# A sixth slot in the ring of split weights, and splitting five units ahead, in a two-layer hybrid decoder on one core

## The reference, cut to what matters

```python
for layer in range(2):
    h = rms_norm(x, attn_norm)
    proj = h @ w_in          # 1024 x 7428: pool, diff q k v, stick q k v, forgetting q k v, forget, gates
    o_pool, o_diff, o_sb, o_fox = mixers(proj)        # o_sb: stick-breaking attention
    merged = sum(sigmoid(gate_n + b_gate_n) * (o_n @ w_branch[rows_n]) for n in range(4))
    x = x + merged @ w_out
    h = rms_norm(x, ffn_norm)
    gate, up = split(h @ w_up)                         # 2 * 2816 columns
    x = x + (silu(gate) * up) @ w_down
```

## Time and profile before

| | |
|---|---|
| median of 3 runs | 895.01 us (894.31 to 897.45) |
| the profiled execution, whole | 895.68 us |
| its span, first to last instruction | 892.8 us |
| TensorE busy | 875.3 us, 98% |
| VectorE, ScalarE, GpSimd busy | 611.1, 443.0, 114.4 us |
| mean granted TensorE clock | 0.994 |
| DMA | 160.10 MB, mean 179 GB/s |

### The profile page before, as it was taken

How to read it: one execution, slowest core, us unless ns; L and a number is a source line. 1 busy time by engine, 2 the same in 40 slices (tenths; PEclk the granted TensorE clock), 3 DMA queues, 4 the chain that set the end, 5 groups by cost and what they waited for, 6 DMA issues and landing times.

```text
span 892.8 us, 11371 instructions
## 1 busy us (share of the span) xinstructions
PE 875.3 (98%) x4308; PEld 722.3 (81%) x4308; DVE 611.1 (68%) x902; ACT 443.0 (50%) x635; POOL 114.4 (13%) x89
## 2 busy tenths in 40 slices
PE   7998999999999999999999989999999999999998
PEld 6876888788788888888888878887887888888886
DVE  5799677777967666654478977758687676666542
ACT  5464654654445444443274645546444554444431
POOL 0553000001800010000005510000045000000000
PEclk9999999999999999999999989999999999999999
DMA  8843755475566766555555346454656466666551
GB/s 272 268 124 97 225 165 167 130 236 188 187 194 195 213 186 184 183 183 193 183 165 170 115 124 209 137 181 145 235 180 201 146 213 189 189 188 189 181 196 47
DMA packets 91014, 160.10 MB, mean 179 GB/s; under 512 B 11472, under 2 KB 17744, under 8 KB 90960
## 3 DMA queue, kind: packets, MB, share of 16 engines
q1 hardware_dynamic: 90960, 159.38, 57.3%
HBM read 158.31 MB, written 1.05 MB: 179 GB/s over the span
## 4 chain that ended last, share of the span: by engine, by line
PE 81%; DVE 13%; issue 2%; DMA 1%; ACT 1%; POOL 1%; SPq 0%; POOLq 0%; DVEq 0%; ACTq 0%
PE bulk L1591 24%; PE bulk L1595 24%; PE bulk L1592 24%; DVE w_lo L941 6%; DMA raw<-in_w_in_dram 1%; PE bankAB L1346 1%; POOL wide L667 1%; PE bankT L1486 1%; ACT w_hi L695 1%; DVE wide L1240 1%; DVE stat L1027 1%; DVE wide L1039 1%; PE bankAB L1532 1%; PE bankO L1505 1%; DVE softplus_lo L1110 0%
## 5 line engine op out<-in xcount | busy, mean ns | idle before, releaser
L941 DVE TENSOR_TENSOR w_lo<-raw,w_hi 128x1024 fp32r<-128x1024 f32 (+1 forms) x288 | 368.4, 1289 | 165.9 <-ACT w_hi L695 163.4
L695 ACT ACTIVATE w_hi<-raw 128x1024 fp32r<-128x1024 f32 (+1 forms) x288 | 299.7, 1049 | 259.7 <-PE bulk L1595 232.5
L1591 PE MATMUL bulk<-w_hi,hT_hi 128*128 128x512 f32 (+1 forms) x896 | 354.0, 395 | 3.7 <-DVE w_lo L941 3.6
L1592 PE MATMUL bulk<-w_lo,hT_hi 128*128 128x512 f32 (+1 forms) x896 | 346.8, 387 | 0.0
L1595 PE MATMUL bulk<-w_hi,hT_lo 128*128 128x512 f32 (+1 forms) x896 | 343.7, 388 | 0.0
L1591 PEld LDWEIGHTS bulk<-w_hi,hT_hi 128*128 128x128 f32 x896 | 169.3, 189 | 38.7 <-DVE w_lo L941 5.1
L1595 PEld LDWEIGHTS bulk<-w_hi,hT_lo 128*128 128x128 f32 x896 | 168.7, 189 | 34.6
L1592 PEld LDWEIGHTS bulk<-w_lo,hT_hi 128*128 128x128 f32 x896 | 169.5, 189 | 32.1
L1591 PE MATMUL bulk<-w_hi,aT_hi 128*128 128x512 f32 x176 | 68.8, 391 | 0.0
L1595 PE MATMUL bulk<-w_hi,aT_lo 128*128 128x512 f32 x176 | 68.5, 389 | 0.0
L1592 PE MATMUL bulk<-w_lo,aT_hi 128*128 128x512 f32 x176 | 68.5, 389 | 0.0
(11 more groups left out here) (240 smaller groups left out, 737.1 us busy)
## 6 DMA issues: line engine op xcount, KB each, us to landing
raw<-in_w_in_dram SPq DMA_DIRECT2D x112, 512.0 KB, 4.0
raw<-in_w_ffn_up_dram SPq DMA_DIRECT2D x80, 512.0 KB, 4.4
raw<-in_w_ffn_down_dram SPq DMA_DIRECT2D x44, 512.0 KB, 3.3
raw<-in_w_branch_dram SPq DMA_DIRECT2D x20, 512.0 KB, 3.3
raw<-in_w_out_dram SPq DMA_DIRECT2D x16, 512.0 KB, 3.2
bias<-in_b_gate_dram SPq DMA_DIRECT2D x16, 256.0 KB, 4.0
raw<-in_w_ffn_up_dram SPq DMA_DIRECT2D x16, 256.0 KB, 3.1
raw<-in_w_in_dram SPq DMA_DIRECT2D x8, 256.0 KB, 2.6
```

The lines of the kernel that those rows point to most:

```text
L695: act.activation(w_hi[:, g % RING, :, 0:width], raw[:, g % RAW, :, 0:width], ACT.Copy).then_inc(hi_ready, 1)
L941: vec.tensor_tensor(w_lo[:, g % RING, :, 0:width], raw[:, g % RAW, :, 0:width], w_hi[:, g % RING, :, 0:width].bitcast(F32), ALU.subtract). ...
L1591: pe.matmul(dst, hi, whi, start=(k == ks[0]), stop=False)
L1592: pe.matmul(dst, hi, wlo, start=False, stop=False)
```

## The change

The ring of `w_hi` and `w_lo` gets a sixth slot, and ACT and DVE split five units ahead of TensorE. `raw` stays at four slots.

```diff
 RAW = 4
-RING = 5
-AHEAD = 4
+RING = 6
+AHEAD = 5
 WARM_UP = 50
```

## The result

| | before | changed |
|---|---|---|
| median, 5 runs each on the same chip | 894.69 us (890.12 to 897.45) | 900.51 us (900.03 to 902.64) |
| the profiled execution, whole | 895.68 us | 900.03 us |
| its span | 892.8 us | 898.2 us |
| mean granted TensorE clock | 0.994 | 0.990 |

The account below looks back on a forecast made before the run. DVE's queue was taken to set the pace in the first 81 us; 4.8 + 2.0 + 0.4 - 1.7 = 5.5 us on the median of 895.01 gave 900.5 us, bounds 897.4 to 903.5.

Parts of the forecast that it names:

- The bound: In the first 81 us DVE's queue, not TensorE's, sets the pace; TensorE has some 2.7 us of slack.
- Steady part: After start-up, each split waits for the same event; 0.8 us of split waits move to `softplus_lo`, so the value is 0.
- First term: At the start, unit 8 must arrive before the first `dq` norm, held back by SP's queue: 4.8 us later.
- Second term: Layer 0 behind the `dq` norm: GpSimd's rotation slows DVE's splits, 2.0 us more, bounds 0 to 2.9.
- Third term: TensorE's clock: `sb_scores(0)` partly at half clock, +0.4 us; the fall at 82 us goes, -1.7 us.
- The wait near 38: TensorE waits some 1.5 to 2 us for unit 9's `w_lo`, not added to the sum.
- Rival 2: Faster: the deeper ring thins DVE's queue ahead of `softplus_lo`, both waits shrink, 8 us less, 887 us; chance 0.04.

Follow-up runs that it names:

- e9: The kernel before (five slots, four ahead), with DVE's low split of step 17 put off behind `softplus_lo` in both layers; 889.64 us, ratio 0.9946.
- e6: e2 with DVE's low splits of step 17 (both layers) and step 16 (layer 1) put off behind `softplus_lo`; 886.95 us, ratio 0.9915.
- e2: The changed kernel with six slots but four units ahead up to step 29 of layer 0, then five; 895.47 us, ratio 1.0021.
- e1: The changed kernel with the sixth slot kept and both engines back at four units ahead; 892.56 us, ratio 0.9983.
- e3: The changed kernel with unit 8's load issued ahead of four parameter loads; 899.17 us, ratio 1.0047.
- e5: The changed kernel with GpSimd rotating only one of eight `dq` heads in both layers, one execution; 893.76 us.
- e7: The changed kernel with four units ahead up to step 3, then five, so unit 8 is split behind the `dq` norm; 897.76 us, ratio 1.0043.
- e4: The changed kernel with the 768 KB of pooling bands loaded at unit 12 instead of unit 3; 900.34 us, ratio 1.0062.
- e10: e9 with the pooling bands loaded at unit 12 and the five casts of constants at step 3; 888.84 us, ratio 0.9942.
- e11: e6 with the pooling bands loaded at unit 12 and the five casts of constants at step 3; 885.84 us, ratio 0.9904.

## Why the prediction held, step by step

- **The bound.** That DVE's order and not TensorE sets the pace ahead of the two stages was right: e9 differs from before, and e6 from e2, by nothing else than splits moved behind `softplus_lo`, and both gain.
- **Steady part, 0.** Right in the profiled executions. In the changed kernel the lateness is 5.75 us at L974 of layer 1 and 5.77 at `sb_sums(1)` (525.23 - 519.46). The waits on `w_lo` went over into `softplus_lo`, which became 2.97 where 2.6 had been said. But e2 beside e1 shows a loss of 2.9 us for the lead of five in the later part, in the medians; the prediction has no term for it, and in which waits it lies stays open.
- **First term, 4.8.** Right in kind: 29.25 - 25.40 = 3.85 us. It is 1.0 smaller, since the load flew 6.84 us and was issued 0.3 earlier. The reason given for its lateness isn't borne out. I had said that SP's own queue held it back; in e3's profiled execution it was issued 3.2 us earlier and didn't land earlier. What does set its landing stays open.
- **Second term, 2.0.** Right in kind, measured 2.98 (from L974 to the end of `keys_lo` 23.04 us against 20.06). The piece up to the first split grew by 1.17, the four splits by 2.66 and the casts by 1.06, and what follows shrank by 1.91: five splits at 1.8 to 1.9 us had been said, and it was four at 1.97 and the fifth, at 49.18, at 1.2. I had taken half of the casts' 1.82 us as removable; they took 2.88. The value of the upper bound, 2.9, would have been right. The two mis-sizings, -1.0 and +1.0, cancel, so the closeness of the sum is partly luck; and since this stretch varies by 3 us between traces of one order, 2.98 is itself one draw.
- **Third term, +0.4 - 1.7.** `sb_scores(0)` ran at a clock of 0.60 (54 to 62 us) and `sb_sums(1)` is late by 88.68 - 81.27 = 7.41 us against 6.84 for `sb_scores(0)`: +0.57. The fall behind `sb_sums(1)` is gone: clock 1.00 over 87 to 92 us, and where the earlier trace rows has 0.66 as well: -1.7. From the steps: 3.85 + 2.98 + 0.57 - 1.7 = 5.7, and 5.5 had been forecast. The span grew by 5.4 and the median by 5.8.
- **The wait near 38.** It came, 1.35 us, but on L1039 and not on unit 9's `w_lo`: unit 8's matmuls need the bank that the `dq` norm reads, and the norm was late too. I had priced only the split. It lay in the cover of the wait at `sb_scores(0)`, so it cost nothing.
- **The rivals.** Rival 2 had the right place and the wrong actor: taking splits from in front of `softplus_lo`, with the late lead, does give some 8 us (887 had been said, e6 took 886.95), but the change doesn't do it and the order has to.

## What to carry to other kernels

When engines work through a fixed order, running one step further ahead brings nothing in the steady part if the event that releases each step is the same (here it even cost some 3 us beside the same ring with a lead of four). At the start it puts one more load in front of the first stage, and if that stage is on the path, the kernel is late from there to its end. First see what the matrix engine waits for: if it is a stage in the helper's queue and not the look-ahead work itself, spend the spare slot on putting look-ahead work off behind that stage. And when a stage is moved in time, see which other engine's work it now lies beside.

## What was not expected of the hardware

- A 512 KB load issued 3.2 us earlier into the same traffic was under way for 10.4 us instead of 6.84 (e3); the medians of the weight loads of this size in the changed kernel are 3.3 to 4.3.
- The same five casts on DVE took 1.0 us in e5, where GpSimd has little to do, 1.8 before, 2.9 in the changed kernel and 4.2 in e7. The order alone doesn't settle it: e1 and e6, both with the start of before, have 1.1 and 4.2. That it goes by which GpSimd instructions they meet fits e5 and is argued for the rest.
- The same wait of TensorE doesn't always bring the same clock. After 2.97 us at `sb_sums(1)` of layer 1 the clock over the next 8 us was 0.57 in the changed kernel and 1.00 in e4. In layer 0, after 3.00 us at the same place, it was 1.00 in e5 (82.8 to 88 us) and 0.58 in e7 (84.4 to 92 us). Waits below 1 us, as in e10 and e11, were followed by no fall there. One such fall is worth 3.4 us, more than half of what was to be explained here, so a single execution can't tell these versions apart.
